# A two-block transformer kernel: POOL makes the convolution's diagonals, and the memory attention's steps are ordered anew

## The reference

```
h = x
hn = rms_norm(h)
proj = hn @ w_in
a, gate = proj[:768] + b, proj[768:1536] + b;  q_mem = proj[1536:]
u = a * sigmoid(gate)
c = depthwise_conv(u, 31 taps, causal) + dw_b       # 768 channels
c = silu(layer_norm(c))
m = memory_attention(q_mem)        # 4 heads, 256 memory rows
h = h + concat(c, m) @ w_out
h = h + swiglu(rms_norm(h))        # width 2816
```

## Time and profile before

| | |
|---|---|
| median of 3 runs | 2330.68 us (2329.95 to 2336.1) |
| the profiled execution | 2334.36 us, its span 2332.4 us |
| mean granted TensorE clock | 0.982 |
| busy: PE, DVE, ACT, POOL | 2244.3, 1726.8, 1427.8, 45.1 us |

### The profile page before, as it was taken

How to read it: one execution, slowest core, us unless ns; L and a number is a source line. 1 busy time by engine, 2 the same in 40 slices (tenths; PEclk the granted TensorE clock), 3 DMA queues, 4 the chain that set the end, 5 groups by cost and what they waited for, 6 DMA issues and landing times.

```text
span 2332.4 us, 36712 instructions
## 1 busy us (share of the span) xinstructions
PE 2244.3 (96%) x11906; PEld 1917.4 (82%) x11906; DVE 1726.8 (74%) x2310; ACT 1427.8 (61%) x1965; POOL 45.1 (2%) x35
## 2 busy tenths in 40 slices
PE   7889998999999999999999999799989999998998
PEld 7779986788888888888888888688779878877987
DVE  6756656569898989898989899765576546557654
ACT  5454444448787878787777788544545434454543
POOL 0000005000000000000000000000000000000000
PEclk9999999999999999999999999899999999999999
DMA  5225554049999999999999999756146555524654
GB/s 212 82 90 192 184 188 142 10 182 363 356 355 357 356 351 364 346 363 342 370 352 361 371 344 369 285 181 196 58 155 196 190 180 172 190 73 157 196 189 145
DMA packets 152640, 557.80 MB, mean 239 GB/s; under 512 B 16912, under 2 KB 17040, under 8 KB 152336
## 3 DMA queue, kind: packets, MB, share of 16 engines
q1 hardware_dynamic: 152032, 554.53, 66.6%
q10 hardware_dynamic: 432, 1.02, 0.1%
HBM read 554.44 MB, written 1.05 MB: 238 GB/s over the span
## 4 chain that ended last, share of the span: by engine, by line
PE 83%; issue 7%; DVE 4%; ACT 4%; DMA 1%; POOL 0%; SPq 0%; DVEq 0%; ACTq 0%; POOLq 0%
PE L L1658 64%; PE L L1711 8%; PE TB L1726 2%; PE L L1675 2%; PE SC L2021 1%; PE L L1824 1%; ACT diag L697 1%; PE SC L2029 1%; DVE cacc L1172 1%; ACT SMX L634 1%; DMA raw<-w 1%; ACT whi L542 1%; PE L L1720 1%; DVE wlo L926 1%; ACT hn L634 1%
## 5 line engine op out<-in xcount | busy, mean ns | idle before, releaser
L926 DVE TENSOR_TENSOR wlo<-deep,whi 128x1024 fp32r<-128x1024 f32 x675 | 795.8, 1222 | 57.7 <-ACT whi L542 39.3
L542 ACT ACTIVATE whi<-deep 128x1024 fp32r<-128x1024 f32 x675 | 706.0, 1060 | 124.5 <-PE L L1658 118.5
L926 DVE TENSOR_TENSOR wlo<-raw,whi 128x1024 fp32r<-128x1024 f32 x368 | 445.9, 1226 | 295.4 <-ACT whi L542 289.2
L542 ACT ACTIVATE whi<-raw 128x1024 fp32r<-128x1024 f32 x368 | 384.0, 1058 | 363.3 <-PE L L1658 242.5
L1658 PE MATMUL L<-whi,xhi 128*128 128x512 f32 (+1 forms) x1392 | 548.5, 394 | 4.2 <-issue 3.2
L1658 PE MATMUL L<-whi,xlo 128*128 128x512 f32 (+1 forms) x1392 | 541.4, 389 | 0.0
L1658 PE MATMUL L<-wlo,xhi 128*128 128x512 f32 (+1 forms) x1392 | 541.2, 389 | 0.0
L1658 PEld LDWEIGHTS L<-whi,xhi 128*128 128x128 f32 x1392 | 261.8, 188 | 61.6 <-DVE wlo L926 5.7
L1658 PEld LDWEIGHTS L<-whi,xlo 128*128 128x128 f32 x1392 | 261.8, 188 | 55.2
L1658 PEld LDWEIGHTS L<-wlo,xhi 128*128 128x128 f32 x1392 | 262.1, 188 | 51.8
L1658 PE MATMUL L<-whi,mhi 128*128 128x512 f32 x448 | 175.9, 393 | 0.0
(11 more groups left out here) (321 smaller groups left out, 3001.0 us busy)
## 6 DMA issues: line engine op xcount, KB each, us to landing
deep<-wm SPq DMA_DIRECT2D x679, 512.0 KB, 5.6
raw<-w SPq DMA_DIRECT2D x368, 512.0 KB, 3.9
mbuf<-mem SPq DMA_DIRECT2D x2, 1024.0 KB, 8.5
const<-const SPq DMA_DIRECT2D x1, 1312.0 KB, 9.0
out<-hn SPq DMA_DIRECT2D x2, 512.0 KB, 2.6
h<-x ACTq DMA_DIRECT2D x1, 512.0 KB, 4.9
h<-x SPq DMA_DIRECT2D x1, 512.0 KB, 4.7
mbuf<-gfin SPq DMA_DIRECT2D x1, 512.0 KB, 4.4
```

The lines of the kernel that those rows point to most:

```text
L542: act(whi[:, p % SLOTS, :], slots[:, slot, :], ACT.Copy).then_inc(w.s.hi, 1)
L926: v.tensor_tensor(wlo[:, p % SLOTS, :], slots[:, (p - first) % len(loaded), :], whi[:, p % SLOTS, :].bitcast(F32), ALU.subtract).then_inc( ...
```

## The change

POOL makes all 78 diagonals, each as a product of the identity by a scalar per partition, ahead of the power of the memory's norm; it starts when the constants are loaded. ACT's loops lose them and keep only the splits. In the memory attention ACT does the first pair's exponentials ahead of the silus, the silus within the hook of the first two steps, the second pair's exponentials behind them, and the splits later; DVE does its `clo` differences and splits in a hook of the same steps; PE's output panels are moved one step later, with one of them behind the loop. Eight of DVE's taps move ahead of the wait for the memory's chunk. Two warm-ups are shortened.

```diff
--- before.py
+++ after.py
@@ -491,7 +491,18 @@
                 w.n["h"] += 1
 
             w = Walk(e, A)
+            def diagonals(c):
+
+                for i in range(TAPS_PE):
+                    for k in (2 * c, 2 * c + 1):
+                        ins = e.tensor_scalar(diag[k][:, i, :], ident, sp("dww", k * TAPS + TAPS_V + i, 1), None, ALU.mult)
+                ins.then_inc(s_diag, 1)
+
             row(w)
+            e.wait_ge(s_in[0], 16)
+            e.wait_ge(s_in[1], 16)
+            for c in range(3):
+                diagonals(c)
             row(w)
             heads(w, 4)
             heads(w, 4, 48)
@@ -615,7 +626,7 @@
                             ).then_inc(w.s.hact, 1)
                 w.n["k"] += len(groups)
 
-            def attention(w, pairs, slots, out=output_bank, between=lambda s: None):
+            def attention(w, pairs, slots, out=output_bank, between=None):
 
                 plan = score_slots(slots)
 
@@ -656,15 +667,19 @@
 
                 steps = steps_of([x[0] for x in pairs])
                 exps(0)
-                between(-1)
-                exps(1)
+                ahead = 2 if between is None else 1
+                if between is None:
+                    exps(1)
+                else:
+                    between(-1)
                 for s in range(len(steps) + 2):
-                    between(s)
                     if s < len(steps):
                         i, j, _ = steps[s]
                         copies(i)
-                        if j == 0 and i + 2 < len(pairs):
-                            exps(i + 2)
+                    if between is not None:
+                        between(s)
+                    if s < len(steps) and j == 0 and i + ahead < len(pairs):
+                        exps(i + ahead)
                     if s >= 2 and steps[s - 2][2]:
                         pair_out(steps[s - 2][0])
                 w.n["a"] += len(pairs)
@@ -690,14 +705,6 @@
                 if q < 2:
                     split_to(w, q + 2)
 
-            def diagonals(c, begin, end):
-
-                for i in range(begin, end):
-                    for k in (2 * c, 2 * c + 1):
-                        ins = act(diag[k][:, i, :], ident, ACT.Copy, scale=sp("dww", k * TAPS + TAPS_V + i, 1))
-                if end == TAPS_PE:
-                    ins.then_inc(s_diag, 1)
-
             def sigmoids(c):
 
                 complete(w)
@@ -712,11 +719,7 @@
             chunk(w, 4, last)
             sigmoids(0)
             for c in (1, 2):
-                w.n["p"] += 4
-                for step in range(4):
-                    split_to(w, w.n["p"] + LOOK - 3 + step)
-                    diagonals(c - 1, step * TAPS_PE // 4, (step + 1) * TAPS_PE // 4)
-                w.n["g"] += 1
+                chunk(w, 4, last)
                 sigmoids(c)
                 if c == 1:
                     e.wait_ge(s_in[3], 16)
@@ -725,9 +728,6 @@
                                 accum_out=norm_cols(w)[:, t:t + 1])
                     i.then_inc(w.s.nss, 1)
                     w.n["n"] += 1
-            for step in range(4):
-                diagonals(2, step * TAPS_PE // 4, (step + 1) * TAPS_PE // 4)
-                split_to(w, w.n["p"] + 2 + (step + 1) // 2)
             w.n["p"] += 2
             w.n["g"] += 1
             head_squares(w, ((s_ev, 4), [(z[:, :, 0:256], PT[:, 0, 0, :].rearrange("p (t n) -> p t n", t=T))]))
@@ -742,14 +742,24 @@
             for c in range(3):
                 e.wait_ge(s_cen, c + 1)
                 act(u[:, 2 * c:2 * c + 2, 0:S], cacc[:, 2 * c:2 * c + 2, :], ACT.Square).then_inc(s_lsq, 1)
-            for c in range(3):
+            def silus(c):
+
                 e.wait_ge(s_lsc, c + 1)
                 for k in (2 * c, 2 * c + 1):
                     act(chi[:, k, :], cacc[:, k, :], ACT.Silu, scale=sp("lng", k, 1), bias=sp("lnb", k, 1))
                     i = act(cacc[:, k, :], cacc[:, k, :], ACT.Silu, scale=sp("lng", k, 1), bias=sp("lnb", k, 1))
                 i.then_inc(s_lhi, 1)
-            attention(w, [(1, False, None, 6 + i) for i in range(2)], SLOTS_MEM, lone_output,
-                      lambda s: split_to(w, w.n["p"] + 4 + max(s + 1, 0)) if s < 3 else None)
+
+            def between(s):
+
+                if s < 0:
+                    silus(0)
+                elif s == 0:
+                    silus(1)
+                    silus(2)
+                else:
+                    split_to(w, w.n["p"] + min(2 * s + 2, 8))
+            attention(w, [(1, False, None, 6 + i) for i in range(2)], SLOTS_MEM, lone_output, between)
             w.n["p"] += 8
             w.n["g"] += 2
             for q in range(2):
@@ -1219,7 +1229,7 @@
                 split_to(w, min(w.n["p"] + 2 + q, w.n["p"] + 4))
                 if q == 2:
                     taps(2)
-            taps(6)
+            taps(14)
             banks = settled(w, 4)
             e.wait_ge(w.s.nr, 2)
             for t in range(T):
@@ -1258,11 +1268,23 @@
             for c in range(3):
                 v.tensor_tensor(cacc[:, 2 * c:2 * c + 2, :], cacc[:, 2 * c:2 * c + 2, :],
                                 TB[1][:, 0:S].unsqueeze(1).to_broadcast([P, 2, S]), ALU.mult).then_inc(s_lsc, 1)
-            for c in range(3):
+            def lows(c):
+
                 e.wait_ge(s_lhi, c + 1)
                 v.tensor_tensor(clo[:, 2 * c:2 * c + 2, :], cacc[:, 2 * c:2 * c + 2, :],
                                 chi[:, 2 * c:2 * c + 2, :].bitcast(F32), ALU.subtract).then_inc(s_llo, 1)
-            attention(w, memory, SLOTS_MEM, lone_output, None, lambda s: split_to(w, w.n["p"] + 4 + s))
+
+            def between(s):
+
+                if s == 0:
+                    lows(0)
+                elif s == 1:
+                    lows(1)
+                    lows(2)
+                else:
+                    split_to(w, w.n["p"] + 2 * s)
+            attention(w, memory, SLOTS_MEM, lone_output, None, between)
+            split_to(w, w.n["p"] + 8)
             banks = settled(w, 6)
             add_rows(w, banks, 0, s_h)
             w.n["p"] += 2
@@ -1868,7 +1890,7 @@
             e.drain().then_inc(A.pv, 2)
             w = Walk(e, A)
             e.wait_ge(s_in[0], 16)
-            warm(5, SC[0])
+            warm(3, SC[0])
 
             def taps(c, begin, end):
 
@@ -1919,7 +1941,7 @@
             for t in range(T):
                 ins = mm(TB[1][:, t * P:(t + 1) * P], ones, sg[:, 0, t * P:(t + 1) * P], start=True, stop=True)
             ins.then_inc(s_rall, 1)
-            warm(6, TB[0])
+            warm(4, TB[0])
             def out_panel(c, j):
 
                 e.wait_ge(w.s.lo, w.at("p", 1 + SLOTS))
@@ -1937,16 +1959,18 @@
             def out_panels(s):
 
                 if s == 0:
-                    e.wait_ge(s_llo, 1)
-                    out_panel(0, 0)
-                    e.wait_ge(s_llo, 2)
-                    out_panel(0, 1)
-                if s == 1:
+                    e.wait_ge(s_lsc, 3)
+                elif s == 1:
+                    for j in range(2):
+                        e.wait_ge(s_llo, j + 1)
+                        out_panel(0, j)
+                elif s == 2:
                     e.wait_ge(s_llo, 3)
                     out_panel(0, 2)
-                if s >= 2:
-                    out_panel(1, s - 2)
+                else:
+                    out_panel(1, 0)
             placed = attention(w, memory, SLOTS_MEM, lone_output, None, out_panels)
+            out_panel(1, 1)
             placed(1)
             out_panel(0, 3)
             out_panel(1, 2)
```

## The result

The changed kernel takes 2318.18 us (median of five, 2317.58 to 2321.96) where the kernel before, run beside it, takes 2332.17 (2329.95 to 2336.1). The ratio is 0.9938, with a 95% interval of 0.9927 to 0.995: faster by 14.0 us. The forecast was 2317 us, within 2312 to 2326. The sum behind it holds in its large terms; three of its terms turned out to hang on a clock that the same instructions do not always get, and part of the closeness of the total is luck.

A forecast was written before the change was run, and what follows sets the result against it. PE, busy for 96% of the span, bounds the kernel, so time comes only from where it stands or runs slowly. -1.6 - 2.6 - 6.8 - 1.2 - 2.4 + 1.0 = -13.6 us, giving 2317 us, range 2312 to 2326.

The forecast's parts named there:

- warm-up: At the start: shortening the first warm-up from 5 to 3 gives -1.6 us, or 0 if PE's clock comes up later.
- `taps(0)`'s wait: Chunk 0: with diagonals ready, PE's 2.60 us wait for ACT's last diagonal goes and `taps(0)` starts at 37.7; -2.6 us.
- turn of `mbuf`: Memory's chunk: ends 15.9 us after the narrow chunk's end instead of 20.6, PE's clock held across a 2.5 us wait.
- contention of +1: DVE beside POOL: a DVE instruction meeting POOL loses 0.14 us on average, 0.42 at most; charged +1 us (0 to 8).
- `taps(14)` and statistics: From the memory's chunk through the means: eight taps moved ahead of DVE's wait, statistics at full clock (-1.2 us); together -3.3.
- exponentials and panels: Memory attention: first exponentials ahead of the silus, output panels and splits later; -2.4 us (0 to -3).
- A diagonal on POOL: POOL's 128x128 product: taken as 0.5 us, all 78 done near 55 to 60, covered up to 0.92 us each.
- POOL's lateness: Rival: memory norm's power late behind 78 diagonals; whole gain gone at 1.1 us each, near 2367 at 1.56; chance 0.06.
- the lock: Rival: DVE and POOL exclude each other; the narrow chunk ends 5 to 8 us later, 2324 us; chance 0.13.
- The clock falls: Rival: fewer warm-ups and thin work cost about 2 us at each place, together +5, 2322 us; chance 0.11.
- DVE was the real bound: Rival: ACT's freedom only lets DVE show; only moved taps and two PE waits count, 2323.5 us; chance 0.08.
- half clock at 14, 70 or 119 us: Sign that would make the prediction wrong: a granted clock of 0.5 at any of these times.

The follow-up runs named there:

- e12_best_again: The same kernel as e10, run and profiled once more; 2316.70 us, ratio 0.9921 to the kernel before.
- e2: The kernel before with only the memory attention's new order, its warm-ups left at 5 and 6; 2331.12 us, ratio 0.9986.
- e3: The kernel before with only eight more of DVE's taps ahead of the wait for the memory's chunk; 2329.29 us, ratio 0.998.
- e7: The changed kernel with 26 extra products on POOL, into an unread tile, ahead of the third chunk's diagonals; 2332.40 us, ratio 0.9999.
- e6: The changed kernel with the third chunk's 26 diagonals made by ACT in its idle time, POOL making 52; 2317.13 us, ratio 0.993.
- e10: The changed kernel with ACT making the third chunk's diagonals and six warm-up rows before the third turn of the memory's chunk; 2319.11 us, ratio 0.9939.
- e9: The changed kernel with six more PE warm-up rows between the second and third turn of the memory's chunk; 2318.27 us, ratio 0.9933.
- e11: The changed kernel with the memory attention's order as before and the short warm-ups kept; 2324.13 us, ratio 0.9962.
- e4: The changed kernel with both warm-ups as long as before; 2320.92 us, ratio 0.995.
- e8: The changed kernel with the eight taps back behind the memory's chunk; 2323.84 us, ratio 0.9956.

## Why the prediction was right, by its own steps

Forecast and measured, in the profiled pair:

| term | forecast | after against before | what the other runs add |
|---|---|---|---|
| warm-up | -1.6 | 0 | -1.6 in six of nine profiles |
| `taps(0)`'s wait | -2.6 | -2.7 (at N) | see below |
| turn of `mbuf` (N to C), contention of +1 in it | -3.7 | -2.6 | -3.4 with POOL quiet and the clock low, -4.9 with it kept |
| `taps(14)` and statistics (C to P) | -3.3 | -4.1 | some -6 where the clock falls behind the old wait |
| exponentials and panels | -2.4 | -2.5 | order 2.2, the rest the second warm-up |
| sum | -13.6 | -12.0 | |

The prediction's -6.8 is parted here at C: the chunk of the memory from N + 20.6 to N + 15.9 is -4.7, and with the +1 for POOL -3.7; the -2.1 left of it and the -1.2 of the statistics stand in the row of C to P.

*Warm-up: the step that failed in the profiled execution.* The turn starts at 10.68 as worked out. But the panels near 15 us run 0.21 apart, and the third turn of `hn` begins at 18.69 (18.58 before). The same stretch of e12_best_again, with the same PE instructions:

```profile
10.70 1.38 PE L1754 MATMUL TB<-const,hn 128*128 128x128 f32 x8
13.55 0.66 PE L1754 MATMUL TB<-const,hn 128*128 128x128 f32 x4 [1.46 <-DVE xlo L990]
...
14.28 0.29 PE L1739 MATMUL L<-xlo,whi 128*128 128x256 f32 x1
14.40 0.28 PE L1739 MATMUL L<-xhi,whi 128*128 128x256 f32 x1
...
16.92 0.60 PE L1754 MATMUL TB<-const,hn 128*128 128x128 f32 x4
```

Here they start 0.12 apart, even behind a longer wait, and `taps(0)` starts at 37.51, where the prediction put it. The prediction's lower bound ("worth 0, if PE's clock then comes up later") was the case drawn. With it the stage would have given -12.0 - 1.6 = -13.6, the forecast sum, but only because the turn of `mbuf` (1.1 short) is made up by the taps with the statistics (0.8 over) and smaller terms. The 14.0 us between the medians are near the 13.6 by luck in part: in the profiled pair 2.7 us of the difference lie behind R, of which the prediction said nothing.

*The wait of `taps(0)`.* It is gone, but 2.6 us is not its steady price. In e2 and e3, whose code is the same up to there, it was 0.9 and 1.7 us. The 1.6 us in which ACT waited for a panel at 33 us, which the prediction set aside as hidden, was 0.0 and 0.7 there: ACT's diagonals stood behind it and so it was on the path. With diagonals made elsewhere a late panel costs nothing at that place: ACT waited 2.0 us once for a panel in the changed kernel, and `taps(0)` started without a wait. Either way the change starts `taps(0)` at 37.5 to 39.4 in place of 39.8 to 41.9.

*A diagonal on POOL: mis-sized.* 0.615 us by its median and 0.82 on average stand in place of 0.5, so the 78 end at 73.9 and not by 60, inside the 0.92 us that the cover allowed. e7 shows that the cover is real.

*DVE beside POOL.* The charge of 1 us was right in size: `xlo` is 0.8 us later at N. The Trainium skill, SBUF — State Buffer, "Who interferes with whom", would have the later of the two fully blocked. Which engine pays changes within the execution. Beside DVE's splits POOL pays: the diagonal that starts at 21.37 us takes 2.54 us, the three splits there 3.59 where 3.49 is their time alone. From 43.4 to 51 us POOL pays beside taps too: a diagonal takes 0.84 us, and twenty taps in 8.37 us lose almost nothing (0.42 each, 0.41 in the earlier trace rows). From 64.3 to 68.9 us DVE pays: nine diagonals take 0.61 us each, and the eight taps lose 1.3 us, 0.16 each, where waiting out a diagonal each time would cost some 0.6. So the trace agrees where POOL pays and disagrees on the size of what DVE pays, and N did not move by the rival's 5 to 8 us. The changed kernel's views of lines 498 and 1182 (least, median and longest in ns), from 43.4 to 51 us and then from 64.33 to 68.89:

```profile
L498 POOL TENSOR_SCALAR diag<-const,small x10: 841/842/844, 43.4 to 50.8; 128x128 f32<-128x128 f32 x10
L1182 DVE SCALAR_TENSOR_TENSOR cacc<-u,small,cacc x20: 470/488/561, 42.9 to 50.8; 128x256 f32<-128x256 f32 x20
...
L498 POOL TENSOR_SCALAR diag<-const,small x9: 602/609/611, 64.2 to 68.8; 128x128 f32<-128x128 f32 x9
L1182 DVE SCALAR_TENSOR_TENSOR cacc<-u,small,cacc x8: 490/657/659, 64.3 to 68.2; 128x256 f32<-128x256 f32 x8
```

*The turn of `mbuf`: mis-sized by the clock.* N to C is 17.8; the forecast's N + 15.9 for the chunk's end is 15.7 at the row of C. The third turn is 0.9 us late (4.4 us after N, not 3.5), and the turn with its 12 panels takes 4.7 us (72.19 to 76.92), where e7 took 3.3 (69.74 to 73.00); 0.3 of these 2.3 us are won back before C. The argument that a gap of 2.6 us keeps the clock rested on one gap in one execution; e6 and e7 show it going either way. With POOL quiet and rows in the gap (e10, e12) N to C is 15.5, just under the forecast.

*`taps(14)`.* DVE waited 0.9 us for the chunk of the memory, where it was to arrive late, and both engines meet at the means as forecast. The term was under-sized by what the clock does behind a wait of 2.7 us.

*The rivals.* POOL's lateness and the lock did not come. "The clock falls" came at the start and at the third turn and cost 1.6 + 1.4 us. Behind the means the kernel before had two stretches at 0.50 (118.9 to 122.3 and 125.8 to 129.1 us), the changed kernel has one (116.4 to 119.7), under the second scores and the warm-up, and the sums ahead of it run at 1.00. "DVE was the real bound" is partly there: DVE keeps 0.4 of e9's 1.5 us.

*The signs.* The prediction named half clock at 14, 70 or 119 us as a sign of being wrong, and in the changed kernel PE ran slowly up to 17.4 us and the granted clock was 0.50 from 72.0 to 75.3 and from 116.4 to 119.7; it also named taps over 0.6 us, which seven of 102 reached. These were poor signs: the sum stood in spite of them, because the first two stretches cost 1.6 and 1.4 us of 13.6. The 78 products did not end by 60. The wait for `exps(1)` (1.41 us) and the missing wait for `cacc` came as said. The last output panel ends at 152.1 us (164.1 before), not near 149, which had left out the charge for POOL.

*What stays open.* Why one execution keeps the clock over a gap and the next does not, and whether the 2.7 us behind R, and e11's slower runs, belong to chance alone; fourteen profiles give a spread of 9 us there and no order by kernel.

## What to carry to other kernels

A chain that PE waits for is shortened best by giving its side work to an idle engine, but count what waits behind that engine's queue: here 0.82 of 0.92 us per product were used, and doubling a third of the work lost the whole gain. A short wait on PE costs its length plus a possible half-clock stretch behind it, so eight taps moved by one number gave 4 to 7 us for a wait of 2.7. And judge a small edit by the distance between landmarks in the stage that it touches. C to P is 30.64 or 30.65 us in five profiles (after, e3, e4, e6, e11), and e10 and e12, one kernel, have every landmark within 0.2 us of each other. The first landmark itself is drawn within 2 us, and untouched layers moved the total by more than the small edits did.

## What the runs showed of the hardware

POOL's 128x128 product in float32 takes 0.598 us at the least and up to 2.535 beside DVE's splits, against 1.56 for 128x512: 0.25 of the elements for 0.38 of the time. PE's panels near 15 us ran slowly in the changed kernel while the view of that window reads a granted clock of 1.00:

```profile
13.70:17.20 3.50, 3.50 (x17) 3.50 (x18) 3.49 (x6) 2.39 (x5) 3.50 (x4) 1.00 0.70 259
```

This 1.00 is no reading. The trace's record of the clock begins at 17.36 us in this execution, just where the spacing of the matmuls falls from 0.21 to 0.12 us, and the view takes what lies ahead of the record as full. In the two other profiles that start `taps(0)` late with the short warm-up (e8, e9) the record begins at 17.36 and 17.48 us, in the six that start it early between 11.3 and 13.3. In e12_best_again, where it begins at 11.34, a window of nearly the same length holds 31 matmuls:

```profile
13.55:17.20 3.65, 3.65 (x31) 3.65 (x32) 3.64 (x6) 2.38 (x5) 3.65 (x5) 1.00 0.81 297
```
